# Pool products half a unit later in the mixing stage, and another order of high halves, copies and low halves in the MLP's first group

## The reference, cut to what matters

```python
# first block, per layer: "mixing"
a = banded_attention(q, k, v, rel_bias, sink) * silu(g_a)
p = multiscale_pool(u_p, pool_w, pool_scale) * silu(g_p)   # 4 groups of 128 channels, windows 2, 4, 8, 16
mixed = concat([a, p]) @ w_out
x = x + rmsnorm(mixed, post_norm_g)
...
# multiscale_pool, per group: centred mean of the window minus the token, then a 128x128 product
y = mean_window(u) - u
y = (y @ pool_w[g]) * pool_scale
...
# second block, its end: the MLP
h2 = rms_norm(x, norm2_g)
u = square(relu(h2 @ w_up))
x = x + u @ w_down
```

## Time and profile before

| what | value |
|---|---|
| median of 3 runs | 2249.12 us (2248.92 to 2251.27) |
| the profiled execution | 2251.29 us, its span 2249.5 us |
| PE busy | 2183.2 us, 97% of the span |
| DVE, ACT, POOL busy | 1429.5, 862.5, 984.0 us |
| granted TensorE clock, mean | 0.992 of full |
| the mixing stage | 256.0 to 334.0 us of the span |
| group 0 of the MLP | 1629.4 to 1667.4 us |

### The profile page before, as it was taken

One profiled execution on the slowest core, in us unless ns is written; L12 is line 12 of the kernel. 1 busy time (PEld: TensorE's weight loads), 2 busy tenths in 40 slices (PEclk: granted clock), 3 DMA queues, 4 the chain that ended last, 5 costly groups with the idle time before them and its releaser, 6 DMA issues. The chain is left out here.

```text
span 2249.5 us, 29130 instructions
## 1 busy us (share of the span) xinstructions
PE 2183.2 (97%) x10530; PEld 1814.4 (81%) x10530; DVE 1429.5 (64%) x2460; ACT 862.5 (38%) x1577; POOL 984.0 (44%) x716
## 2 busy tenths in 40 slices
PE   7999989999999999999999999999989999999999
PEld 7788777778887888888888788888868888787887
DVE  6776673605543666666666474332777887899795
ACT  5455423300002555555555321211454545534332
POOL 3232445535453223132231355447465655655554
PEclk9999999999999999999999999999999999999999
DMA  6320114122335233233332365224125445827433
GB/s 222 101 71 22 43 42 173 73 87 75 107 110 144 80 97 90 80 108 84 91 97 74 122 217 186 85 75 168 66 84 178 150 159 181 305 88 254 136 105 120
DMA packets 195544, 267.17 MB, mean 119 GB/s; under 512 B 57896, under 2 KB 113736, under 8 KB 195440
## 3 DMA queue, kind: packets, MB, share of 16 engines
q1 hardware_dynamic: 118272, 189.59, 24.6%
q10 hardware_dynamic: 77168, 76.19, 10.9%
HBM read 190.19 MB, written 83.95 MB: 122 GB/s over the span
## 5 line engine op out<-in xcount | busy, mean ns | idle before, releaser
L159 POOL TENSOR_TENSOR w_hi<-w_raw,zero 128x512 fp32r<-128x512 f32 x216 | 259.0, 1230 | 913.3 <-PE ps L204 792.8
L204 PE MATMUL ps<-a_hi,w_hi 128*128 128x512 f32 x1408 | 547.2, 409 | 8.0 <-PEq L1666 3.2
L204 PE MATMUL ps<-a_hi,w_lo 128*128 128x512 f32 x1408 | 526.3, 394 | 0.0
L204 PE MATMUL ps<-a_lo,w_hi 128*128 128x512 f32 x1408 | 524.1, 393 | 0.0
L204 PE MATMUL ps<-w_hi,a_hi 128*128 128x512 f32 (+1 forms) x1088 | 420.4, 386 | 10.3 <-POOL w_lo L2625 2.7
L204 PE MATMUL ps<-w_lo,a_hi 128*128 128x512 f32 (+1 forms) x1088 | 418.3, 384 | 0.0
L204 PE MATMUL ps<-w_hi,a_lo 128*128 128x512 f32 (+1 forms) x1088 | 418.3, 384 | 0.0
L204 PEld LDWEIGHTS ps<-a_hi,w_lo 128*128 128x128 f32 x1408 | 266.3, 189 | 59.5
L204 PEld LDWEIGHTS ps<-a_hi,w_hi 128*128 128x128 f32 x1408 | 266.9, 190 | 52.0 <-issue 10.1
L204 PEld LDWEIGHTS ps<-a_lo,w_hi 128*128 128x128 f32 x1408 | 267.7, 190 | 42.9
L164 POOL TENSOR_TENSOR w_lo<-w_raw,w_hi 128x512 fp32r<-128x512 f32 x216 | 288.0, 1365 | 4.2
(11 more groups left out here) (257 smaller groups left out, 3496.4 us busy)
## 6 DMA issues: line engine op xcount, KB each, us to landing
w_raw<-in_w_in_dram SPq DMA_DIRECT2D x32, 1024.0 KB, 5.2
mlp_part<-u_parts SPq DMA_DIRECT2D x26, 1024.0 KB, 8.1
feat_fm<-stage ACTq DMA_DIRECT2D x68, 256.0 KB, 2.1
u_parts<-mlp_acc SPq DMA_DIRECT2D x28, 512.0 KB, 2.9
u_parts<-res SPq DMA_DIRECT2D x28, 512.0 KB, 2.7
conv_in<-feat_fm ACTq DMA_DIRECT2D x24, 512.0 KB, 6.0
qkv_tm<-stage_tm ACTq DMA_DIRECT2D x5, 2048.0 KB, 6.9
res<-in_x_dram SPq DMA_DIRECT2D x16, 512.0 KB, 6.3
```

Of the source, the lines that this page charges most:

```text
L159: hi = nc.gpsimd.tensor_tensor(w_hi[slot][:, k:k + 2, :], w_raw[:, k:k + 2, :], zero[:, 0:1].unsqueeze(2).to_broadcast([P, 2, CW]), ALU.add)
L204: last = nc.tensor.matmul(out_of(o), lhs, rhs(o), start=first and n == 0, stop=final and n == 2)
```

## The change

In `phase_mix` a unit and its copy can be made by halves. PE runs the first half of unit 2 before pool product 0, and its second half and the first half of unit 3 before pool product 1, which then stands before the second half of unit 3. ACT makes y_high(0) between the two halves of u_high(1), and y_high(1) between the two halves of u_high(2).

In the MLP's group 0 ACT makes the high half of m6's weights before m6's operand in place of after copy 2; then, after copy 2, two of the four blocks of m7's operand, the high half of m7's weights (with a new wait for m5's product, whose weights it overwrites), the other two blocks, copy 3 and finish 0, where before m7's operand, finish 0, copy 3 and the weights of m7 followed each other. DVE makes the low halves of m7's operand before add 1, not after it. The other groups keep their order.

```diff
                     unit(0)
                     unit(1)
+                    unit(2, (0,))
                     pool_product(0)
-                    unit(2)
+                    unit(2, (1,))
+                    unit(3, (0,))
                     pool_product(1)
-                    unit(3)
+                    unit(3, (1,))
                     out_part(0)
...
                     u_high(0)
                     silu(5)
                     silu(4)
-                    u_high(1)
+                    u_high(1, (0,))
                     y_high(0)
-                    u_high(2)
+                    u_high(1, (1,))
+                    u_high(2, (0,))
                     y_high(1)
+                    u_high(2, (1,))
                     for j in range(4):
                         high_a(j)
...
                         if first:
+                            act.wait_ge(combined, 4)
+                            up_high(0, "m6")
                             operand_high("m6")
                         copy(i, 2, tile)
+                        if first:
+                            operand_high("m7", (0, 1))
+                            act.wait_ge(combined, 5)
+                            act.wait_ge(mm_p, 3)
+                            up_high(0, "m7")
+                            operand_high("m7", (2, 3))
+                            copy(0, 3, tile)
+                            finish(0, 0, tile)
+                        else:
+                            if not last:
+                                act.wait_ge(combined, i * 5 + 4)
+                                up_high(i, "m6")
+                            finish(i, 0, tile)
+                            copy(i, 3, tile)
+                            if not last:
+                                act.wait_ge(combined, i * 5 + 5)
+                                up_high(i, "m7")
                         if not last:
-                            act.wait_ge(combined, i * 5 + 4)
-                            up_high(i, "m6")
-                        if first:
-                            operand_high("m7")
-                        finish(i, 0, tile)
-                        copy(i, 3, tile)
-                        if not last:
-                            act.wait_ge(combined, i * 5 + 5)
-                            up_high(i, "m7")
                             finish(i, 1, tile)
...
                         up_sum(nc.vector, "m7")
-                        add(i, 1, tile)
                         if first:
                             operand_low(2, "m7")
-                        else:
+                        add(i, 1, tile)
+                        if not first:
                             part_sums(i - 1, ("m6", "m7"), quarters(i - 1))
```

More of the change, by code:

```diff
@@ L1165, in _, with unit @@
                 def _(pe):
-                    def unit(i):
+                    def unit(i, halves=(0, 1)):
                         fb, slot = order[i] % 2, slot_of(W_U1 + i // 2)
@@ L1170, in unit @@
                             pe.wait_ge(u_out, 2 * i - 2)
-                        for half in range(2):
+                        for half in halves:
                             for k in range(KB):
@@ L1218, in silu, with u_high @@
                         nc.scalar.activation(res[:, j, :], res[:, j, :], ACT.Silu).then_inc(silued, 1)
-                    def u_high(i):
+                    def u_high(i, halves=(0, 1)):
                         if i >= 2:
                             act.wait_ge(u_free, i - 1)
-                        for half in range(2):
+                        for half in halves:
                             act.wait_ge(mm_u, 2 * i + half + 1)
@@ L2691, in up_high, with operand_high @@
                         nc.scalar.activation(up_quarter(w_hi, p, last), up_raw(p), ACT.Copy).then_inc(w_high, 1)
-                    def operand_high(p):
-                        for t in range(4):
+                    def operand_high(p, tiles=(0, 1, 2, 3)):
+                        for t in tiles:
                             act.wait_ge(p_sum, TURNED_SUMS.index((p, t)) + 1)
```

## The result

The changed kernel takes 2235.57 us (median of 4 runs, 2232.2 to 2238.04), the kernel before 2249.33 in the same comparison: a ratio of 0.9935, 95% interval 0.9924 to 0.9947. The forecast was 2231.8 us, range 2229.0 to 2238.0; the median lies in the part of the range that the prediction had given to its rival A (2234.5 to 2238), not in that of its own sum (2229 to 2234.5). Three runs further down, of 2577, 4728 and 4960 us, are in a second, slower state and are left out of the ratios; the medians, which count them, would move by about 0.4 us at most without them.

What follows compares the result with a forecast made beforehand. PE, busy nearly throughout, was taken as the bound, losing time to stalls and half clock behind them. Gains of 11.3 (mixing) and 6.0 us (MLP), together 17.3, gave 2231.8 us from a median of 2249.12; range 2229.0 to 2238.0.

Steps and rivals of the forecast that it cites:

- rival A: MLP gain partly given back by half clock behind short gaps, turns, or late product 1: 2234.5 to 2238 us, chance 0.18.
- its own sum: Mixing-stage gain 11.3 plus MLP gain 6.0 us, giving 2231.8 us; its range 2229 to 2234.5, chance 0.66.
- 11.3: Mixing stage: gain in us if no stall is left, 6.3 idle and 5.0 half clock and pipeline start.
- m6: MLP group 0: POOL finishes m6's weights at 1644.7, before m1 ends, so PE's 1.33 us wait goes.
- at the row's pace of 4.46 us for four: MLP group 0: DVE's four low halves for m7, beside POOL, take 4.46 us and end at 1652.3.
- ends at 1644.48 + 3.31 = 1647.8, before and after: MLP group 0: DVE's sum for m7's weights takes 3.31 us, its end unmoved by the change.
- exclusive lock: MLP group 0: DVE and POOL take turns at a shared port pair; m7 starts near 1654.3, 0.7 us later.
- I put no half clock there: MLP: the clock stays up behind m7's 2.3 us idle gap, so no half-clock cost is counted.
- the row of 2.17: Profile row before the change: a 2.17 us PE stall with a 0.47 us first matmul behind it, clock not fallen.
- B: One half of the change gives nothing because another chain ends as late: 2238 (MLP) or 2243 us (mixing), chance 0.10.
- C: The change does not do what it says, or later barriers take back the gain: 2247 to 2251 us, chance 0.03.
- D: Slower: from MLP group 1 on, each of seven groups idles before m2; 2264 us, chance 0.03.

Runs made afterwards that it cites:

- mlp_only: The kernel before with only the change's MLP part, mixing stage as before: 2246.4 us, ratio 0.9978.
- mlp_act: The kernel before with only ScalarE's new order in the MLP, VectorE and mixing stage as before: 2246.27 us, ratio 0.9982.
- both_early: The changed kernel with four more moves in MLP group 0 (sums, copy 3 and weights made earlier): 2229.81 us, ratio 0.9907 to the kernel before.
- pool_waits: The changed kernel, POOL's low half of m7's weights in group 0 waiting for all low halves of m7's operand: 2232.62 us, ratio 0.9917.
- again1: The changed kernel run once more, nothing else changed: 2234.82 us, ratio 0.9924 to the kernel before.
- the two parts: mix_only and mlp_only, each half of the change alone against the kernel before: 11.5 and 5.2 us less.
- mix_first: The changed kernel with TensorE moving only pool product 0; product 1 again between whole units 2 and 3: 2245.04 us, ratio 0.9976.
- mix_only: The kernel before with only the change's mixing-stage part, MLP as before: 2240.13 us, ratio 0.9951.
- mlp_dve: The kernel before with only VectorE's new order in the MLP, ScalarE and mixing stage as before: 2247.73 us, ratio 0.9982.

## Why the prediction was right, and where it was not

**The mixing stage.** Right by its own steps. out_part(0) was to start 11.3 us earlier; 314.60 against 303.40 us is 11.2. Product 0 was forecast at 283.3 (283.37) and product 1 at 295.6 (295.65). y_low(1) was to be through at 293.1 to 295.0. The changed kernel's DVE:

```profile
292.02 1.21 DVE L1313 TENSOR_TENSOR mix_y_lo<-mix_y,mix_y_hi 128x1024 fp32r<-128x1024 f32 x1
```

That is 293.2, a margin of 2.4 us. What I had as one figure, 11.3, is partly chance: with its stalls the stage of the old order took 58.57 us in the first trace, but 55.59 in mlp_only's and 57.39 in mlp_act's, as the half clock behind them was longer or shorter (in mlp_only the clock stayed up behind the 3.42 us before product 0); the new order takes 47.33 to 47.35 in each of its traces.

**m6.** Right: its wait is gone.

**m7 and m2.** The chain was right, the size was 0.7 us off: m7 was put at 1653.65. Counted from the group's first matmul (1629.37 before) it came at 24.96, that is 1654.33 on the old count; m2 at 32.67, that is 1662.04 for 1661.35. The step that failed is the term "at the row's pace of 4.46 us for four". In that row POOL stopped after 2.93 us, so only two of the four were slowed. In the new place three were, as the changed kernel's window on them shows (us, busy of DVE with these instructions, PEclk, DMA):

```profile
1637.60:1642.77 5.17, 5.10 (x3) 1.00 0.68 201
```

The three took 1.7 us each, the fourth, with POOL through, 0.68, together 5.79 us, 1.3 more than the term. Part of that was made good by a second miss: "ends at 1644.48 + 3.31 = 1647.8, before and after" was 0.5 us too late for the sum of m7's weights, which took 2.4 us now and not 3.31, one of its two instructions being slowed and not both. The gain to m2 was 5.3 and not 6.0 us. By the exclusive lock that the Trainium skill states ("SBUF — State Buffer", section "SBUF: two separate sides") the prediction had m7 at 1654.3. The trace agrees with turns, one instruction of each engine per 1.7 us, against 0.6 and 1.2 us from start to start where one works alone. That the place was met to 0.1 us is luck, though: the prediction had the third and the fourth low half slowed; it was the first three, from an earlier start. That the low halves' new place before add 1 would matter was implied in my chain; mlp_act shows that it does not.

**The clock.** This is where the rest went. "I put no half clock there" was the step for the gaps of 2.3 and 2.2 us, by the row of 2.17, and it failed: by the prediction's own list it would be wrong if the clock fell behind the short gaps, and it did. Rival A had the fall, at 1.7 to 2.9 us each. In the first trace the clock fell behind m2's gap (1.5 us) and behind the 2.18 us between the stages, which no rival of mine named, since it had not fallen there before and I took that gap as unchanged. By the rows of the fall itself, ten matmuls from 325.00 on take 3.95 us where at the pace of the others they take 2.4: 1.55 us. From out_part(0) to the MLP's first matmul the changed kernel then took 1316.33 us against 1314.77 before, 1.6 more, and 11.2 - 1.6 + 5.3 - 1.5 is 13.4 us, against 13.3 between the spans.

That the 1.6 us are the stage end's fall can be checked, for the same stretch, which no edit touches, took 1312.0 us in both_early and 1318.4 in pool_waits. PE stands idle in it for 22.2 to 22.7 us in all ten traces; what differs is where the clock was down. Between 674 and 701 us it was down twice in every trace. Behind a wait of 3.22 us near 1270 it was down in eight of ten, and up in again1 and both_early. The first trace and again1 behind that wait:

```profile
1268.00:1273.00 5.00, 4.84 (x12) 3.80 (x13) 0.06 (x1) 0.00 (x0) 4.77 (x5) 0.50 0.29 79
```

```profile
1269.00:1274.00 5.00, 5.00 (x22) 4.16 (x23) 0.04 (x1) 0.00 (x0) 4.92 (x5) 1.00 0.30 77
```

The changed kernel took 1316.33 us with this fall and 1313.6 without it (again1), so it costs about 2.8 us; both_early, without the stage end's fall too, took 1312.0. pool_waits had this fall and two more, behind 2.09 us near 371 and 1.82 us near 457. The kernel before and the first trace of the changed kernel both had the fall near 1270 and differ in the stage end's alone, so the 1.6 us are that one.

The forecast of 17.3 us was thus 0.8 too much in its two stages, whose gain by the marks is 16.5 us. The other 2.7 us between this and the median of the four runs, 13.8 us less than before, is the size of one or two falls. In the first trace, 13.3 us less between the spans, the two falls of 1.6 and 1.5 us account for all of the rest; in the other three runs no trace tells. That the medians of again1 and of the two parts give 16.8 and 16.7 proves little, as their traces hold falls as well, and so do the runs of before: the intervals of the two comparisons of the changed kernel, 0.9924 to 0.9947 and 0.9911 to 0.9938, overlap. So the mechanism was right in both stages, and that the time fell inside the range, in its upper part, is owed to the share left for A. B, C and D are out: both halves gain, nothing is taken back, and the groups from 1 on move with PE.

## What to carry to other kernels

When the bound engine waits for a short chain of other engines, look first for its own independent work that can be cut in half and put ahead of the wait, and then for what stands in front of the chain in another engine's list; here y_high(0), held back for 2.1 us (276.4 to 278.57), was part of a stall of 3.4 us with half clock behind it. In this kernel a gap of about 2 us or more on TensorE cost its idle time and, in some executions, 1.5 to 2.8 us of half clock; so compare traces by the distance between two marks on TensorE and by the granted clock between them, not by the total. When two engines slow each other, try to let the one whose result is needed first go alone: here one wait more shortened the chain.

## What the runs showed of the hardware that I had not expected

The clock can fall behind an idle stretch of TensorE and need not, from execution to execution of the same program, and this over a wide range of lengths. It fell behind as little as 1.8 us (pool_waits near 457, mix_first near 460) and stayed up behind 3.2 us (again1 and both_early near 1270) and 3.42 us (mlp_only before product 0). The 2.2 us between the mixing stage and the next were followed by half clock in the traces of the changed kernel, of again1 and of mlp_only, and by the full clock in those of the kernel before, mix_only, both_early, mix_first, mlp_act, mlp_dve and pool_waits. The wait of 2.8 to 2.9 us before m7 was followed by it in again1 and mlp_only, not in the changed kernel's first trace nor in mlp_act. What decides it within an execution stays open; no run here varied it alone. It shows in the totals: of 25 runs of the kernel before, the one of 2247.17 us had a mean granted clock of 0.994, the one of 2257.45 us 0.990.

A subtraction on DVE and one on POOL, both from two operands in SBUF, slow each other. Four of DVE alone took 2.49 us and two of POOL 2.51; from start to start that is 0.6 and 1.2 us each. Beside each other both engines went at one instruction per 1.7 us, a little under the sum of the two.
